# Six of eight chunk pairs by block products in the up stages of a feed-forward, mixer, feed-forward block

## The reference

```python
def swiglu(h, w_gate, w_up, w_down):
    return (jax.nn.silu(h @ w_gate) * (h @ w_up)) @ w_down
...
h = swiglu(rmsnorm(x, ffn1_pre_g[l]), ffn1_w_gate[l], ffn1_w_up[l], ffn1_w_down[l])
x = x + 0.5 * rmsnorm(h, ffn1_post_g[l])
```

## Time and profile before

| | |
|---|---|
| median of 3 runs | 1826.41 us (1826.05 to 1826.48) |
| profiled execution, its own time | 1826.47 us |
| its span, first to last instruction | 1824.7 us |
| busy: PE, DVE, ScalarE, GpSimd | 99%, 71%, 49%, 3% of the span |
| granted TensorE clock, mean | 0.996 of full |
| DMA | 345.36 MB, 189 GB/s over the span |

### The profile page before, as it was taken

The page is one execution under the profiler, slowest core; times in us unless marked ns, Lnnn a source line. Parts: engine busy times, 40 slices in busy tenths (PEclk is TensorE's granted clock), DMA queues, the critical chain, the costliest instruction groups (busy, mean ns, idle before and its releaser), DMA issues.

```text
span 1824.7 us, 20137 instructions
## 1 busy us (share of the span) xinstructions
PE 1799.3 (99%) x8226; PEld 1493.4 (82%) x8226; DVE 1300.0 (71%) x1333; ACT 896.5 (49%) x1003; POOL 53.2 (3%) x111
## 2 busy tenths in 40 slices
PE   7899999999999999999999999999999999999998
PEld 6788888888888888888888887888888888888886
DVE  4788888888865544765754547888889888755544
ACT  3655455455644433654234446545555555644432
POOL 0000000000000000170000000000000000000000
PEclk9999999999999999999999999999999999999999
DMA  7466666666666566665443665666666666665563
GB/s 254 127 196 194 210 196 189 211 200 193 199 211 193 197 193 191 196 186 171 134 142 117 209 194 162 193 210 197 196 197 197 195 198 205 217 193 192 195 196 128
DMA packets 150652, 345.36 MB, mean 189 GB/s; under 512 B 10568, under 2 KB 11152, under 8 KB 150176
## 3 DMA queue, kind: packets, MB, share of 16 engines
q1 hardware_dynamic: 149712, 339.79, 59.2%
q0 software_dynamic: 736, 4.26, 0.7%
q10 hardware_dynamic: 112, 0.03, 0.0%
HBM read 341.94 MB, written 2.10 MB: 189 GB/s over the span
## 4 chain that ended last, share of the span: by engine, by line
PE 95%; DVE 2%; ACT 1%; issue 1%; DMA 0%; DVEq 0%; POOLq 0%; POOL 0%; ACTq 0%
PE ps L1152 25%; PE ps L1154 25%; PE ps L1153 25%; PE ps L1346 5%; PE ps L1348 5%; PE ps L1347 5%; PE ps L1457 1%; PE ps L1301 1%; DVE wlo L716 1%; ACT xT_hi L438 0%; ACT whi L380 0%; PE ps L1494 0%; ACT xT_hi L418 0%; DVE xT_lo L779 0%; PE ps L1286 0%
## 5 line engine op out<-in xcount | busy, mean ns | idle before, releaser
L716 DVE TENSOR_TENSOR wlo<-raw,whi 128x1024 fp32r<-128x1024 f32 x520 | 626.5, 1225 | 345.7 <-ACT whi L380 343.8
L380 ACT ACTIVATE whi<-raw 128x1024 fp32r<-128x1024 f32 x520 | 542.1, 1058 | 526.1 <-DMA raw<-in_ffn_w_down_dram 241.6
L1152 PE MATMUL ps<-whi,xT_hi 128*128 128x512 f32 x1248 | 494.1, 396 | 15.1 <-DVE wlo L716 13.9
L1154 PE MATMUL ps<-whi,xT_lo 128*128 128x512 f32 x1248 | 487.8, 391 | 0.0
L1153 PE MATMUL ps<-wlo,xT_hi 128*128 128x512 f32 x1248 | 487.2, 390 | 0.0
L1152 PE MATMUL ps<-whi,hT_hi 128*128 128x512 f32 x832 | 324.2, 390 | 0.0
L1154 PE MATMUL ps<-whi,hT_lo 128*128 128x512 f32 x832 | 323.8, 389 | 0.0
L1153 PE MATMUL ps<-wlo,hT_hi 128*128 128x512 f32 x832 | 323.7, 389 | 0.0
L1152 PEld LDWEIGHTS ps<-whi,xT_hi 128*128 128x128 f32 x1248 | 235.2, 188 | 68.6 <-issue 17.0
L1154 PEld LDWEIGHTS ps<-whi,xT_lo 128*128 128x128 f32 x1248 | 235.1, 188 | 49.9
L1153 PEld LDWEIGHTS ps<-wlo,xT_hi 128*128 128x128 f32 x1248 | 235.4, 189 | 46.6
(11 more groups left out here) (154 smaller groups left out, 1661.1 us busy)
## 6 DMA issues: line engine op xcount, KB each, us to landing
raw<-in_ffn_w_down_dram SPq DMA_DIRECT2D x176, 512.0 KB, 4.6
raw<-in_ffn_w_gate_dram SPq DMA_DIRECT2D x116, 512.0 KB, 3.7
raw<-in_ffn_w_up_dram SPq DMA_DIRECT2D x116, 512.0 KB, 3.6
raw<-in_w_in_dram SPq DMA_DIRECT2D x80, 512.0 KB, 3.6
raw<-in_w_out_dram SPq DMA_DIRECT2D x32, 512.0 KB, 4.1
srawB<-in_ffn_w_up_dram SPq DMA_DIRECT2D x30, 512.0 KB, 3.8
srawB<-in_ffn_w_gate_dram SPq DMA_DIRECT2D x30, 512.0 KB, 4.7
srawA<-in_ffn_w_up_dram SPq DMA_DIRECT2D x30, 512.0 KB, 3.8
```

Of the source, the lines that this page charges most:

```text
L380: nc.scalar.activation(whi[:, slot(g), :], raw[:, slot(g), :], ACT.Copy).then_inc(hi_ready, 1)
L716: V.tensor_tensor(wlo[:, slot(g), :], raw[:, slot(g), :], whi[:, slot(g), :].bitcast(f32), ALU.subtract).then_inc(lo_ready, 1)
L1152: mm(bank, a_hi, whi[:, s, c0:c0 + NT], start=start, stop=False, skip_group_check=skip)
L1154: return mm(bank, a_lo, whi[:, s, c0:c0 + NT], start=False, stop=stop, skip_group_check=skip)
```

## The change

- Six pairs (0 to 5) by block products in the ten later tiles, two (6, 7) plainly.
- Weight sums on GpSimd (`weight_sums`), in the same three dependent instructions for each pair, and the token sums too (`token_sums`, in two parts of three pairs).
- Loads go to two staging buffers `stg` (4 x 512 columns); GpSimd, ScalarE and DVE read them from there and write three operand areas A, B, C. A staging buffer is loaded again when GpSimd has made the sums and DVE the low parts.
- Plain halves in the later tiles have two ring slots in place of four.
- The gated product goes to DRAM in each tile and comes back in the down stage, where PE transposes it; `hT` is gone, and high and low parts are made straight from PSUM.

```diff
-PAIRS = (0, 1, 2)
-PLAIN = 5
-NS = len(PAIRS)
+NS = 6
+PLAIN = KC // 2 - NS
...
         if b + 16 <= g < d:
-            return (g - b) % 4
...
+            return (g - b) % 2
...
 def area(q):
-    return (q + 1) % 2
+    return (q + 1) % 3
...
+    stg = [at("stg0", 22, [P, 4, NT]), at("stg1", 54, [P, 4, NT])]
+    sraw = [at("srawA", 88, [P, 7, NT]), at("srawB", 116, [P, 7, NT]), at("srawC", 8, [P, 7, NT])]
...
                 def sums(j, s):
                     q = NS * (j - 1) + s
-                    a = area(q)
+                    dst = stg[q % 2]
                     if q >= 2:
-                        sp.wait_ge(p_done, 7 * (NQ * f + q - 1))
...
+                        sp.wait_ge(s_t, NQ * f + q - 1)
+                        sp.wait_ge(s_blo, NQ * f + q - 1)
...
                 for j in range(1, FTILES):
-                    plain(j, 2)
-                    sums(j, 2)
-                    plain(j, 3)
+                    sums(j, 3)
+                    sums(j, 4)
+                    sums(j, 5)
+                    store_h(f, j - 1)
                     if j < FTILES - 1:
                         sums(j + 1, 0)
-                    plain(j, 4)
+                    plain(j, 1)
                     if j < FTILES - 1:
                         sums(j + 1, 1)
+                        sums(j + 1, 2)
                         plain(j + 1, 0)
-                        plain(j + 1, 1)
+
+            def store_h(f, u):
+                sp.wait_ge(h_ok, 2 * (FTILES * f + u + 1))
+                sp.dma_start(h_d[f][u], flat(gated_h[u % 2][:])).then_inc(h_st[u % 2], 16)
+
+            def load_h(f, u):
+                sp.wait_ge(h_st[u % 2], stored(f, u))
+                if u >= 3:
+                    sp.wait_ge(h_tr, 2 * (FTILES * f + u - 1))
+                sp.dma_start(flat(h_back[back(u)][:]), h_d[f][u]).then_inc(h_in[back(u)], 16)
...
+            def token_sums(f, part):
...
+                link(nc.gpsimd.tensor_tensor(xf[:].rearrange("p n c t -> p (n c) t"), xT_hi[:, k0:k0 + 6, :].bitcast(f32),
+                                             xT_lo[:, k0:k0 + 6, :].bitcast(f32), ALU.add))
+                a11, a12, a21, a22 = (xf[:, :, c, t * P:(t + 1) * P] for t in range(TOK) for c in range(2))
+                link(nc.gpsimd.tensor_tensor(Sf[:, part, 0], a21, a22, ALU.add))
...
+            def weight_sums(f, q):
+
+                w, r = sraw[area(q)], stg[q % 2]
+                pool.wait_ge(s_in[q % 2], 32 * (NQ // 2 * f + q // 2 + 1))
+                if q >= 3:
+                    pool.wait_ge(p_done, 7 * (NQ * f + q - 2))
...
+                link(nc.gpsimd.tensor_tensor(w[:, T3:T1 + 1, :], r[:, 0:1, :].broadcast_to([P, 2, NT]),
+                                             r[:, 1:3, :], ALU.subtract))
+                link(nc.gpsimd.tensor_tensor(w[:, T2, :], r[:, 1, :], w[:, T1, :], ALU.subtract))
+                nc.gpsimd.tensor_tensor(w[:, T4, :], r[:, 3, :], w[:, T2, :], ALU.subtract).then_inc(s_t, 1)
...
-            def block_sums(f, j, s):
+            def block_lo(f, j, s):
 
                 q = NS * (j - 1) + s
...
+                dve.wait_ge(s_bhi, NQ * f + q + 1)
+                V.tensor_tensor(flat(slo[area(q)][:, B22:B21 + 1, :]), flat(stg[q % 2][:, 1:4, :]),
+                                flat(shi[area(q)][:, B22:B21 + 1, :]).bitcast(f32), ALU.subtract).then_inc(s_blo, 1)
...
             def up_tile(b, j):
                 f = 0 if b == U1 else 1
...
+                if j > 1:
+                    gated(b, j - 1)
+                block_lo(f, j, 2)
                 sum_lo(f, j, 2)
+                block_lo(f, j, 3)
+                plain_lo(b, j, 0)
+                block_lo(f, j, 4)
+                sum_lo(f, j, 3)
+                block_lo(f, j, 5)
+                sum_lo(f, j, 4)
+                sum_lo(f, j, 5)
+                lo(b + 16 + 2 * PLAIN * j - 2)
+                if not last:
+                    block_lo(f, j + 1, 0)
+                lo(b + 16 + 2 * PLAIN * j - 1)
...
                 combine(f, j)
...
+                    sum_lo(f, j + 1, 0)
+                    block_lo(f, j + 1, 1)
+                    sum_lo(f, j + 1, 1)
...
                 for j in range(1, FTILES):
-                    for i in range(NS):
-                        plain(b, j, i)
-                        products(f, j, i)
-                    plain(b, j, 3)
-                    hidden(f, j - 1)
-                    plain(b, j, 4)
+                    for s in range(3):
+                        products(f, j, s)
+                    plain(b, j, 0)
+                    for s in range(3, NS):
+                        products(f, j, s)
+                    plain(b, j, 1)
```

More of the change, by code:

```diff
@@ L117, in build @@
     nat = at("nat", 200, [P, TOK, NT])
+    nat1 = at("nat1", 148, [P, TOK, NT])
+    gated_h = [nat, nat1]
+    h_back = [nat1, at("h_odd", 168, [P, TOK, NT]), at("h_even", 172, [P, TOK, NT])]
+    h_d = [nc.dram_tensor(f"gated{f}", (FTILES, P, TOK * NT), f32, kind="Internal").ap() for f in range(2)]
     ident = at("ident", 204, [P, P])
@@ L207, in flat, with block_sum, stored, back @@
             return ap.rearrange("p a b -> p (a b)")
+        def block_sum(ap, part):
+            return ap[:, part].rearrange("p a b c -> p (a b c)")
+        def stored(f, u):
+            return 16 * ((6, 5)[u % 2] * f + u // 2 + 1)
+        def back(u):
+            return 0 if u == 0 else 2 - u % 2
+        def landed(f, u):
+            return 16 * (f + 1 if u == 0 else 5 * f + (u + 1) // 2)
         @block.sync
@@ L366, in _ @@
             inv_root(6, 3, 1, 2)
+            token_sums(1, 0)
+            token_sums(1, 1)
+            weight_sums(1, 0)
             inv_root(7, 4)
+            for q in range(1, NQ):
+                weight_sums(1, q)
             load_gain(D2, g2post_d)
@@ L854, in up_tile @@
[L854 to L870 removed]
+                last = j == FTILES - 1
@@ L872, in up @@
+                if last:
+                    lo(b + UP)
+                combine(f, j)
+                if last:
+                    lo(b + UP + 1)
+                    hidden_lo(f, 0)
+                    gated(b, j)
+                    lo(b + UP + 2)
+                    lo(b + UP + 3)
+                    lo(b + UP + 4)
+                else:
+                    sum_lo(f, j + 1, 0)
+                    block_lo(f, j + 1, 1)
+                    sum_lo(f, j + 1, 1)
             def up(b):
@@ L1332, in first_tile @@
                     narrow_half(b + h, i, ps[2 * m:2 * m + 2])
+                    if not f and m == 0 and i < 6:
+                        transpose_x(i + 2)
             def product(n, q, start):
-                a = area(q)
-                k0 = 2 * PAIRS[q % NS]
+                a, s = area(q), q % NS
+                k0 = 2 * s
                 one, two = slice(0, P), slice(P, 2 * P)
@@ L1353, in products @@
                 q = NS * (j - 1) + s
-                pe.wait_ge(s_lo, 2 * (NQ * f + q) + 2)
-                if q == 0:
-                    pe.wait_ge(sprep_ok, f + 1)
-                if s == 0 and j >= 2:
-                    pe.wait_ge(h_ev, 2 * (FTILES * f + j - 1))
-                for n in (1, 6, 2, 7, 5, 4, 3):
-                    product(n, q, s == 0 and n in (1, 5, 6, 7)).then_inc(p_done, 1)
+                pe.wait_ge(s_blo, NQ * f + q + 1)
+                pe.wait_ge(s_tlo, NQ * f + q + 1)
+                if j == 1 and s in (0, 3):
+                    pe.wait_ge(sprep_ok, 2 * f + s // 3 + 1)
+                if j == 1 and s == 0:
+                    pe.wait_ge(x_lo, KC // 2)
+                    pe.wait_ge(x_sq, 24 if f else 8)
+                if s == 0:
+                    done = 2 * (FTILES * f + j - 1)
+                    for n in (1, 6, 7, 5, 2, 4, 3):
+                        if n in (2, 4):
+                            pe.wait_ge(silu_ok, done + n // 2)
+                        if n == 3:
+                            pe.wait_ge(h_ok, done + 1)
+                        product(n, q, True).then_inc(p_done, 1)
+                else:
+                    for n in (1, 6, 2, 7, 5, 4, 3):
+                        product(n, q, False).then_inc(p_done, 1)
             def plain(b, j, i):
```

361 lines of the change are left out of this document (184 added, 177 removed).

## The result

The changed kernel takes 2121.44 us (2119.73 to 2122.52, 4 runs) against 1826.23 in the same comparison: 1.1616 times as long, with a 95% interval of 1.1596 to 1.1636. The forecast was 2146, in a range of 2050 to 2280; 295.2 us were lost where 320 were forecast. Its profiled execution took 2122.52 us for a span of 2120.6.

A forecast was written before the change was run, and what follows sets the result against it. PE bounds the kernel before; after the change, DVE's and GpSimd's mutually exclusive SBUF reading bounds the tiles. 1826.5 + 302.0 for 20 tiles + 17.4 for transposes in the down stages + 0 gave 2146 us, range 2050 to 2280.

The forecast's parts named there:

- Matmuls, 39.45 us a tile of PE, and DVE's own 34.6: Later tiles: PE needs 39.45 us after saving 2.04 a tile; DVE alone needs 34.6 and would fit under it.
- GpSimd's price, 5.0 us a set: Later tiles: one set of weight sums on GpSimd, undisturbed, takes 5.0 us, six sets 30 us a tile.
- Exclusion in both directions: Later tiles: DVE's two-SBUF-input instructions and GpSimd's SBUF reads shut each other out; 26.7 + 26.9 = 53.6 us a tile.
- A tile of 57.5: Later tiles: 53.6 us of reading, 1.3 of gaps and 2.6 at the end, against 42.4 before; 302.0 us over 20.
- the tile's end: End of each later tile: 2.6 us unused by either engine, while a staging refill runs and DVE does additions.
- First tiles, 0: First tile of each block: 4.0 us won by moving token sums, the 8 given back; bounds -8 and +19.
- Transposes, 17.4 us moved, reload and store 0: Transposes of the gated product move from tiles to down stages, adding 17.4 us there; its DRAM transfers cost 0.
- each with a tile's length to land: 0: Later tiles and down stages: 44 added transfers of 512 KB cost 0, or some 5 us for each late one.
- What it was to look like: Signs in the tiles: longer GpSimd sums and DVE splits, additions still 0.69 us, PE near 70% busy, tiles 55 to 60.
- rival of a falling clock: Later tiles: PE idles about 4 us before each product, its clock drops, total more than 2280 us; chance 0.08.
- PE as the bound: Rival, later tiles: GpSimd's sums fit between DVE's splits, PE sets the tile, total 1786 or 1778 us; chance 0.06.
- Partial exclusion: Rival, later tiles: GpSimd shuts DVE out for half its long instruction, tile 44.1 us, total 1878; chance 0.07.

The follow-up runs named there:

- x_memset: Changed kernel with GpSimd's weight sums replaced by six memsets a set, which write SBUF but read none; 1786.86 us.
- x_copy: Changed kernel with GpSimd's weight sums replaced by copies from the staging buffer, one SBUF input each; 1861.14 us.
- the dose: The pair x_half and x_more, changed kernel with GpSimd's reading in a tile at 13.5 and 40.4 us instead of 26.9; 1895.64 and 2383.79 us.
- b_order: Kernel before the change, with only x transposed and split one pair earlier in the first tile; 1808.88 us, 0.9902 of before.
- x_dve: Changed kernel with all weight sums back on DVE, the token sums still on GpSimd; 2001.49 us.
- b_tok: Kernel before the change, with only the token sums moved to GpSimd, x in the old order; 1825.55 us, 0.9992 of before.
- x_half: Changed kernel with half of GpSimd's weight sums (T3 and T4) replaced by memsets; 1895.64 us.
- x_more: Changed kernel with GpSimd issuing the first sum instruction of each set (1024 columns) twice; 2383.79 us.
- x_mix1: Changed kernel with GpSimd making the weight sums of pairs 1 and 4 only, DVE those of the other four; 2048.86 us.

## Why the prediction was right, step by step

- *Matmuls, 39.45 us a tile of PE, and DVE's own 34.6:* right; x_memset has 39.44 and, in the same window, 34.60.
- *GpSimd's price, 5.0 us a set:* right, 4.9.
- *Exclusion in both directions, the reading of long instructions held whole:* right, shown by the splits' durations, by x_memset, x_copy and the dose. This was the one step beyond the rows, and the turns that the two engines take from 195.76 on bear it out directly. The rule of the Trainium skill ("SBUF — State Buffer", section "Who interferes with whom") that two SBUF inputs on DVE meet GpSimd's reads, and not its writes, agrees with x_memset (2.29, untouched) and x_copy (2.02 instead of 0.61).
- *A tile of 57.5:* 56.2. The 53.6 in which one of the two engines reads while the other is shut out (the port time) and the gaps of 1.3 leave 1.3 where 2.6 were given to the tile's end. GpSimd is hardly ever free: 48.9 busy and 5.85 waiting make up 54.8 of the 55.6 of the tile shown. Its wait for the refill doesn't lie beside DVE's additions, as the 2.6 had it, but after them, from 181.2 to 187.0, where DVE's splits are reading. This is 27 us of the total (302 against 275.4), the largest miss in size.
- *First tiles, 0:* wrong in what it left out. It weighed the token sums and missed the other edit there, x one pair earlier, which b_order shows to be worth 17 us by itself. In the change the first block won 13.4, and the second lost 5.8 (5.7 + 137.8 - 137.7). In the second, token sums and first weight sums stand on GpSimd ahead of the root that the silu needs: its input was there at 1284.5, and it began at 1286.74. But that isn't the main cause. Counted in the same way, the second block loses 4.8 us in x_dve and 4.6 in x_memset too, where GpSimd reads no weights. What these kernels share there (token sums in two parts on GpSimd, the start of the six pairs) wasn't taken apart, so this loss stays open. b_tok says that moving token sums wins nothing, near what was forecast (4 won, 4 lost a block).
- *Transposes, 17.4 us moved, reload and store 0:* the down stages cost 28.1. Nine tiles' transposes came to each down stage, not ten, since one tile's were there before and after the change: those of the first tile now stand at the end of the up stage. 2 x 9 x 0.87 = 15.7. The other 12.4 belong to the step "each with a tile's length to land: 0": PE is idle for 6.8 of them and busy for 5.5 more than the transposes take. At the head of a down stage the step doesn't hold. A weight load issued right behind a reload landed late (chain of waits of the changed kernel, then the timeline of PE, both down stages):

```profile
623.73 9.68 DMA raw<-in_ffn_w_down_dram
...
1857.67 11.74 DMA raw<-in_ffn_w_down_dram
```

```profile
637.01 0.79 PE L1238 MATMUL ps<-whi,hT_hi 128*128 128x512 f32 x1 [2.38 <-DVE hT_lo L868]
...
1873.00 0.80 PE L1238 MATMUL ps<-whi,hT_hi 128*128 128x512 f32 x1 [4.44 <-DVE hT_lo L868]
```

  9.7 and 11.7 us where 4.5 is the median of these loads, then 2.4 and 4.4 us without work on PE, and behind that matmuls 0.43 us apart (637.60 to 639.73) in place of 0.23, the lower clock. The prediction had named 5 us for each late one. GpSimd's load of the gain, 1024 KB, is issued 0.6 us ahead of each of the two late loads; it was there before as well, where the weight loads issued within 5 us of it took 4.4 to 4.8 us in the first block and 4.9 to 8.8 in the second, and PE waited for none of them. New beside it are the reloads and a store of 512 KB each. x_memset, x_half, x_more, x_dve and x_mix1, which keep all of these, have the same late load (9.4 to 12.4 us). Which of these transfers makes it late stays open: leaving out the reload alone, or the gain's load, was not tried.
- *What it was to look like:* GpSimd's and DVE's durations, the additions and the tile as said. PE was to be near 70% busy and was at 83% (46.3 of 55.6): at a granted clock of 0.89 its matmuls took longer. The rival of a falling clock was real in that sense, but the longer matmuls held nobody up in the later tiles: DVE's additions have no idle time before them (0.0 at line 888), and GpSimd waited for PE's products for 11.8 us in the whole program, in two waits. (That rival counted about 4 us of idling before each product; 18 us over six products are 3.)
- *The rivals:* PE as the bound (1786) needed GpSimd not to hold DVE. x_memset is such a kernel, and its 1786.9 agree with 1786 partly by luck: its tiles save 59 us where the rival had 41, its down stages cost 30, and the first tiles give 11 back. Partial exclusion (under 2050) is ruled out by the 2121 and by the turns in the timeline. x_half, with half the reading, is what it would have looked like: 1896 against 1878.

The terms' errors partly cancel: -27 for the tiles, -8 for the first tiles, +11 for the down stages.

## What to carry to other kernels

Before work moves from DVE to GpSimd, add GpSimd's reading time to DVE's time in instructions with two SBUF inputs: in these runs the sum was a floor for the stage, and GpSimd's reading was added to DVE's whole time except where it lay beside DVE's instructions on PSUM or its idle time. Two engines that both look free can be slower together than one of them alone (2121 against 2001). And read all that a change does to the start of a stage: there, one operand prepared a step earlier was worth 17 us, 1%.

## What the runs showed of the hardware that was not expected

- GpSimd's memsets of the same size (0.96 us for 1024 columns, 0.53 for 512) left DVE's splits at 1.75 and 2.29 us; only its reads hold them up, and a copy does so as well as a two-input subtraction.
- The two engines took turns by whole instructions: a 1536-column split on DVE ended 1.61 us after the GpSimd subtraction that it had waited for, which is its reading time of 1.60.
- With GpSimd holding the operand, DVE's instruction shows the wait as its own duration (3.95 us for 1536 columns), so the page counts DVE as busy, and its busy share (75%) doesn't tell that much of it is waiting.
- Loads of 512 KB behind a reload of the same size at the start of a down stage took 9.7 and 11.7 us from issue to landing, with a load of 1024 KB by GpSimd issued 0.6 us ahead of them; with that one but no reload, in the kernel before, weight loads took 4.4 to 4.8 us in the first block and up to 8.8 in the second. Which of the two delays them was not isolated.
